# Norms of 512 tokens by per-token sums: root and reciprocal on 128x4, then spread over all rows by a matmul

## The reference, cut to what matters

```python
def _rmsnorm(x, g):
    x32 = x.astype(jnp.float32)
    y = x32 * lax.rsqrt(jnp.mean(x32 * x32, axis=-1, keepdims=True) + RMS_EPS)
    return y.astype(x.dtype) * g
def _modnorm(x, g_pre, shift, scale):
    return _rmsnorm(x, g_pre) * (1 + scale) + shift
def _residual(x, y, g_post, gate, weight):
    return x + weight * gate * _rmsnorm(y, g_post)
```

## Time and profile before

| | us |
|---|---|
| median of 3 runs | 3153.08 |
| lowest and highest | 3149.70 and 3153.67 |
| the profiled execution | 3148.06 |
| its span, first to last instruction | 3146.4 |
| PE busy in it | 2970.6 (94%) |
| DVE busy | 1012.7 (32%) |
| ACT busy | 448.3 (14%) |
| POOL busy | 393.4 (13%) |
| mean granted clock of PE | 0.981 of full |

### The profile page before, as it was taken

How to read it: one execution, slowest core, us unless ns; L and a number is a source line. 1 busy time by engine, 2 the same in 40 slices (tenths; PEclk the granted TensorE clock), 3 DMA queues, 4 the chain that set the end, 5 groups by cost and what they waited for, 6 DMA issues and landing times.

```text
span 3146.4 us, 27449 instructions
## 1 busy us (share of the span) xinstructions
PE 2970.6 (94%) x10974; PEld 1869.7 (59%) x10974; DVE 1012.7 (32%) x1970; ACT 448.3 (14%) x966; POOL 393.4 (13%) x355
## 2 busy tenths in 40 slices
PE   3999999998899999998999998999889999999998
PEld 1555555554456557443688884656444444888863
DVE  6233324202204633011533235205541002544432
ACT  2000000001103335001210001004430000000011
POOL 0000000000001000001244430000000001444410
PEclk8999999999999999999999999999999999999999
DMA  6233223211110000221122221120002221222211
GB/s 258 81 107 107 94 102 109 101 55 40 54 53 16 22 31 1 70 87 67 67 83 91 84 77 67 67 69 28 28 27 87 71 76 67 81 94 81 94 49 59
DMA packets 42526, 228.17 MB, mean 73 GB/s; under 512 B 4144, under 2 KB 6448, under 8 KB 26928
## 3 DMA queue, kind: packets, MB, share of 16 engines
q1 hardware_dynamic: 32768, 181.17, 17.0%
q0 software_dynamic: 8928, 39.85, 3.5%
q10 hardware_dynamic: 720, 5.61, 0.4%
HBM read 224.51 MB, written 2.10 MB: 72 GB/s over the span
## 4 chain that ended last, share of the span: by engine, by line
PE 91%; DVE 5%; ACT 1%; DMA 1%; issue 1%; POOL 0%; ACTq 0%; DVEq 0%
PE banks L413 57%; PE banks L489 24%; PE banks L601 2%; PE banks L422 1%; DMA consts_sb<-consts 1%; PE banks L773 1%; PE banks L689 1%; PE banks L781 1%; PE banks L926 1%; DVE rstd L1371 1%; DVE p_embed L1421 1%; DVE scratch_b L1388 1%; PE banks L702 1%; PE banks L774 0%; DVE rstd L1381 0%
## 5 line engine op out<-in xcount | busy, mean ns | idle before, releaser
L413 PE MATMUL banks<-normed,weight_ring 128*128 128x512 f32 (+1 forms) x3056 | 1150.4, 537 | 53.4 <-ACT normed L1007 34.0
L413 PEld LDWEIGHTS banks<-normed,weight_ring 128*128 128x128 f32 (+1 forms) x3056 | 582.3, 191 | 610.2 <-issue 564.7
L413 PE MATMUL banks<-big,weight_ring 128*128 128x512 f32 (+2 forms) x1504 | 572.0, 538 | 8.5 <-DVE big L1619 5.6
L413 PEld LDWEIGHTS banks<-big,weight_ring 128*128 128x128 f32 (+2 forms) x1504 | 279.3, 186 | 294.3 <-issue 272.7
L489 PE MATMUL banks<-big 128*128 128x256 f32 x1440 | 331.7, 379 | 0.0
L489 PEld LDWEIGHTS banks<-big 128*128 128x128 f32 x1440 | 273.6, 190 | 37.2
L1984 POOL TENSOR_TENSOR big<-weight_ring 128x512 f32<-128x512 f32 (+1 forms) x64 | 80.0, 1250 | 1176.4 <-PE banks L489 478.3
L489 PE MATMUL banks<-big,weight_ring 128*128 128x256 f32 x840 | 196.3, 379 | 0.0
L489 PEld LDWEIGHTS banks<-big,weight_ring 128*128 128x128 f32 x840 | 159.6, 190 | 21.7
L1421 DVE CUSTOM_DVE_ANT_0 p_embed<-big,rpb_rows 128x1024 f32<-128x1024 f32 x116 | 141.9, 1223 | 22.8 <-DMA big<-w_ada 14.8
L489 PE MATMUL banks<-normed,weight_ring 128*128 128x256 f32 x576 | 136.1, 379 | 0.0
(11 more groups left out here) (286 smaller groups left out, 2407.2 us busy)
## 6 DMA issues: line engine op xcount, KB each, us to landing
weight_ring<-weights SPq DMA_DIRECT2D x136, 1024.0 KB, 4.9
big<-w_ada POOLq DMA_DIRECT2D x42, 512.0 KB, 4.1
weight_ring<-weights SPq DMA_DIRECT2D x20, 768.0 KB, 4.2
weight_ring<-weights SPq DMA_DIRECT2D x16, 704.0 KB, 4.0
big<-w_ada POOLq DMA_DIRECT2D x4, 2048.0 KB, 24.9
rpb_rows<-w_ada POOLq DMA_DIRECT2D x14, 512.0 KB, 4.7
weight_ring<-weights SPq DMA_DIRECT2D x8, 640.0 KB, 3.9
residual<-xT ACTq DMA_DIRECT2D x2, 1536.0 KB, 19.7
```

Of the source, the lines that this page charges most:

```text
L413: ins = nc.tensor.matmul(o, w, r, start=start, stop=stop)
```

## The change

For the seven norms of 512 tokens the sums are turned round: each 128x128 block of squares is the stationary operand and one column of ones the moving one, so that the sums of 128 tokens come out as one column, token on partition, and the four blocks fill four columns. Root and reciprocal then work on 128x4. To get 1/root back onto every row, DVE multiplies the identity by each of the four columns, which makes four diagonal matrices side by side in `DIAG`, and one matmul of ones by `DIAG` puts the value of token t in column t of every row of bank 7 (`spread`). The scaling reads bank 7 in place of `rs`. Norms that cover the context too (two parts) are left as they were.

```diff
+        diag_made, spread_done = sem("rstd_diagonals"), sem("rstd_spread")
+        SPREAD = ("nb_y", "nb_x", "nmix_y", "nmix_x", "nmlp_x", "nple_x", "nfin_x")
@@ PE: sum_squares
+                if len(parts) == 1:
+                    return token_sums(banks[0], SQ[:, k % 2, 0:S], k == 0, k == count - 1)
+            def token_sums(n, rows, start, stop):
+                for c in range(4):
+                    last = nc.tensor.matmul(bank[:, n, c:c + 1], rows[:, c * P:(c + 1) * P], ones[:, 0:1],
+                                            start=start and c == 0, stop=stop, skip_group_check=True)
+                return last
+            def spread(name):
+                pe.wait_ge(diag_made, SPREAD.index(name) + 1)
+                nc.tensor.matmul(bank[:, 7, :], ones, DIAG[:, :, :].rearrange("p c t -> p (c t)"), start=True,
+                                 stop=True).then_inc(spread_done, 1)
@@ PE: out_chunks (and in the same way in out_projection)
-                        for (a, b, _), q in zip(parts, banks):
-                            last = nc.tensor.matmul(bank[:, q, 0:b - a], ones, SQ[:, 1 - j, a:b],
-                                                    start=(peel and j == 1), stop=False)
-                        last.then_inc(sg["sq_used"], 1)
+                        token_sums(banks[0], SQ[:, 1 - j, 0:S], peel and j == 1, False).then_inc(sg["sq_used"], 1)
@@ PE: squares_total
-                nc.tensor.matmul(bank[:, 6, :], ones, SQA[:, 0:S], start=True, stop=False)
-                nc.tensor.matmul(bank[:, 6, :], ones, SQA[:, S:2 * S], start=False, stop=False)
+                token_sums(6, SQA[:, 0:S], True, False)
+                token_sums(6, SQA[:, S:2 * S], False, False)
...
@@ PE: a spread after the sums of each of the seven norms, as in
+            spread("nb_y")
             norm_sums(nb, LAT)
+            spread("nb_x")
@@ ACT: root
+                if len(parts) == 1:
+                    A(rs[:, 0:4], bank[:, banks[0], 0:4], ACT.Sqrt, bias=eps, scale=1.0 / features).then_inc(signal, 1)
+                    return
@@ DVE: norm and post_norm call this, and scale by r in place of rs
+            def inverse_root(parts, name):
+                if len(parts) == 2:
+                    link(V.reciprocal(rs[:, :], rs[:, :]))
+                    return rs
+                link(V.reciprocal(rs[:, 0:4], rs[:, 0:4]))
+                V.tensor_tensor(DIAG[:, :, :], ident.unsqueeze(1).to_broadcast([P, 4, P]),
+                                rs[:, 0:4].unsqueeze(2).to_broadcast([P, 4, P]), ALU.mult).then_inc(diag_made, 1)
+                dve.wait_ge(spread_done, SPREAD.index(name) + 1)
+                return bank[:, 7, :]
```

More of the change, by code:

```diff
@@ L537, in squares_total @@
                 pe.wait_ge(g["added"], 2 * g["turn"] + 2)
-                nc.tensor.matmul(bank[:, 6, :], ones, SQA[:, 0:S], start=True, stop=False)
-                nc.tensor.matmul(bank[:, 6, :], ones, SQA[:, S:2 * S], start=False, stop=False)
+                token_sums(6, SQA[:, 0:S], True, False)
+                token_sums(6, SQA[:, S:2 * S], False, False)
                 pe.wait_ge(g["done"], 4 * g["turn"] + 4)
-                nc.tensor.matmul(bank[:, 6, :], ones, SQB[:, 0:S], start=False, stop=False)
-                nc.tensor.matmul(bank[:, 6, :], ones, SQB[:, S:2 * S], start=False, stop=True).then_inc(g["used"], 1)
+                token_sums(6, SQB[:, 0:S], False, False)
+                token_sums(6, SQB[:, S:2 * S], False, True).then_inc(g["used"], 1)
             def out_projection(g, free, name, tiles, rhs, parts, per_unit, sums):
@@ L555, in out_projection @@
                     pe.wait_ge(sg["sq_used"], sg["base"] + KC - 1)
-                    for (a, b, _), q in zip(parts, banks):
-                        nc.tensor.matmul(bank[:, q, 0:b - a], ones, TMP[:, 0, a:b], start=True, stop=False)
-                    pe.wait_ge(sg["sq"], sg["base"] + KC)
-                    for (a, b, _), q in zip(parts, banks):
-                        last = nc.tensor.matmul(bank[:, q, 0:b - a], ones, SQ[:, 1, a:b], start=False, stop=True)
+                    if len(parts) == 1:
+                        token_sums(banks[0], TMP[:, 0, 0:S], True, False)
+                    else:
+                        for (a, b, _), q in zip(parts, banks):
+                            nc.tensor.matmul(bank[:, q, 0:b - a], ones, TMP[:, 0, a:b], start=True, stop=False)
+                    pe.wait_ge(sg["sq"], sg["base"] + KC)
+                    if len(parts) == 1:
+                        last = token_sums(banks[0], SQ[:, 1, 0:S], False, True)
+                    else:
+                        for (a, b, _), q in zip(parts, banks):
+                            last = nc.tensor.matmul(bank[:, q, 0:b - a], ones, SQ[:, 1, a:b], start=False, stop=True)
                     last.then_inc(sg["sq_used"], 1)
@@ L805, in _ @@
             squares_total(sq2)
+            spread("nmix_y")
             norm_sums(nmix, LAT)
+            spread("nmix_x")
             for b in range(8):
@@ L941, in _ @@
             out_projection(out2, nmlp["xnew"], "out2", KC, MR2, LAT, 16, (nmlp, (6,)))
+            spread("nmlp_x")
             first_up(UP3[0], (V_UP3[1] + 1) % 2, nmlp)
@@ L952, in _ @@
             squares_total(sq3)
+            spread("nple_x")
             pe.wait_ge(p_landed, 16)
@@ L972, in _ @@
                 sum_squares(nfin, o, LAT, (6,)).then_inc(nfin["sq_used"], 1)
+            spread("nfin_x")
         @block.scalar
@@ L1366, in mark, with norm, post_norm @@
                 return chain[0]
-            def norm(g, parts, scale, shifted):
+            def inverse_root(parts, name):
[7 more added lines that the diff above has]
+                return bank[:, 7, :]
+            def norm(g, parts, scale, shifted, name=None):
                 dve.wait_ge(g["root"], g["turn"] + len(parts))
-                width = parts[-1][1]
-                link(V.reciprocal(rs[:, 0:width], rs[:, 0:width]))
+                r = inverse_root(parts, name)
                 for k in range(KC):
                     for a, b, col in parts:
-                        V.scalar_tensor_tensor(H[:, k, a:b], X[:, k, a:b], scale(k, col), rs[:, a:b], ALU.mult,
+                        V.scalar_tensor_tensor(H[:, k, a:b], X[:, k, a:b], scale(k, col), r[:, a:b], ALU.mult,
                                                ALU.mult).then_inc(g["scaled"] if shifted else g["ready"], 1)
-            def post_norm(g, parts, gate_row):
+            def post_norm(g, parts, gate_row, name=None):
                 dve.wait_ge(g["y_root"], len(parts))
-                width = parts[-1][1]
-                link(V.reciprocal(rs[:, 0:width], rs[:, 0:width]))
+                r = inverse_root(parts, name)
                 marks = {}
@@ L1772, in _ @@
             dve.wait_ge(out1["free"], 2 * KC)
-            post_norm(nb, LAT, GATE2)
-            norm(nb, LAT, modulated(SCALE3), True)
+            post_norm(nb, LAT, GATE2, "nb_y")
+            norm(nb, LAT, modulated(SCALE3), True, "nb_x")
             dve.wait_ge(nb["ready"], KC)
@@ L1790, in _ @@
                     add_squares(sq2, m - 1)
-            post_norm(nmix, LAT, GATE3)
-            norm(nmix, LAT, plain("mix_g"), False)
+            post_norm(nmix, LAT, GATE3, "nmix_y")
+            norm(nmix, LAT, plain("mix_g"), False, "nmix_x")
             for b in range(8):
@@ L1917, in _ @@
             residual_adds(nmlp, out2["done"])
-            norm(nmlp, LAT, plain("mlp_g"), False)
+            norm(nmlp, LAT, plain("mlp_g"), False, "nmlp_x")
             XA, XB = X[:, :, 0:HALF], X[:, :, HALF:S]
@@ L1933, in _ @@
                     add_squares(sq3, m - 1)
-            norm(nple, LAT, plain("ple_g"), False)
+            norm(nple, LAT, plain("ple_g"), False, "nple_x")
             for o in range(KC):
@@ L1940, in _ @@
                 V.tensor_tensor(X[:, o, 0:S], X[:, o, 0:S], TMP5[:, s, :], ALU.add).then_inc(nfin["xnew"], 1)
-            norm(nfin, LAT, plain("final_g"), False)
+            norm(nfin, LAT, plain("final_g"), False, "nfin_x")
         @block.gpsimd
```

2 lines of the change are left out of this document (1 added, 1 removed).

## The result

The changed kernel took 3159.23 us (median of 20 executions, 3157.36 to 3163.27), the kernel before 3152.61 (20 executions). The ratio is 1.0023, with a 95% interval of 1.0016 to 1.0030: 6.6 us slower, where 12.0 us faster was forecast.

What follows compares the result with a forecast made beforehand. The prediction took the uncovered root, reciprocal and scaling at seven norms as the bound, with PE busy 94%. Gains of 6.8 + 2.4 + 1.0 + 1.8 = 12.0 us from the median 3153.1 gave 3141 us, range 3131 to 3148.

Steps and rivals of the forecast that it cites:

- What bounds the kernel: At the seven norms of 512 tokens, root, 3.35 us reciprocal and scaling run one by one, 4.11 us at nmlp_x, uncovered.
- The relay, new: Root to scaling at seven norms: 2.42 us at full clock, 3.43 at half, against 4.11; five spreads at half, gain 6.8 us.
- The sums: the price of a pair: On PE, a weight load plus one-column pass takes 0.08 us, so 0.64 us a sum, 0.22 less than a wide one.
- path term: Sums between matmuls of out2 and the last projection: 11 x 0.22, gain 2.4 us (ends 4.0 and -1.1).
- the sums fit under it: In nb_x and nmix_x, sums (0.64, or 0.96 at half clock) fit under DVE's 1.39 us a chunk; gain 1.0 us.
- nmix_y and nple_x: Two small sums follow ACT's square ahead of the root, which starts earlier; gain 0.9 us each, 1.8 us together.
- The stage behind the norm: First matmuls behind norms start earlier but no warmer: 0; ends 5.6 us gained if clock stays up, 2.8 lost.
- The gain is eaten by half speed: Rival: all spreads at half clock, dearer sums, 2.8 us lost behind norms; 1.5 us gain, 3151.6 us, chance 0.07.
- Slower: Rival: in small sums load and pass don't overlap, 0.19 us a pair at full clock, twice at half; 3180 us, chance 0.04.

Runs made afterwards that it cites:

- rsqrt: The kernel before, with root and reciprocal of the seven norms replaced by one ACT instruction for the reciprocal square root; 3118.89 us, ratio 0.9896.
- narrow_loops: The changed kernel with one-column sums only in the loops nb_x and nmix_x and wide sums everywhere else; 3143.99 us, ratio 0.9983 to the kernel before.
- relay_alone: The changed kernel with all sums kept wide, so only root and reciprocal on 128x4, diagonals and spread are new; 3134.74 us, ratio 0.9949 to the kernel before.
- narrow_and_wide: The changed kernel with one unread wide matmul added behind each narrow sum of nb_x and nmix_x; 3177.17 us, ratio 1.0082 to the kernel before.

## Why the prediction was wrong, step by step

The shifts between the two traces, sorted by the terms of the forecast (us, minus is faster):

| term | forecast | measured |
|---|---|---|
| seven relays, root to scaling | -6.8 | -6.2 |
| sums on PE's path | -2.4 | +0.4 |
| loops of nb_x and nmix_x, first sum to root | -1.0 | +6.9 |
| four sums of nmix_y and of nple_x, to the root | -1.8 | +3.0 |
| stages behind the norms | 0 | +3.4 |
| first two chunks of out2 | none | +3.0 |
| sum | -12.0 | +10.5 |

The last term is the scatter named above, and the one before it may hold some too; the medians differ by +6.6.

- *What bounds the kernel* was right: seven reciprocals of 3.35 us on the path, with PE waiting. rsqrt takes them off it and gives 33 us, with the clock behind them.
- *The relay, new.* Forecast 2.42 us at full clock and 3.43 at half; measured 2.49 (nb_y) and 3.36 (nb_x). The small root took 0.26 (0.25 forecast), the reciprocal 0.18 (0.18), the diagonals 0.69 (0.68), the spread with its hand-over 1.17 or 2.11. Right in every term. Six spreads, not five, ran at half clock.
- *The sums: the price of a pair.* I took 0.08 us by L899. L433's loads start 0.11 us apart at full clock (eight fill 0.97, the last of them 0.19 long) and 0.21 at half (25 fill 5.41), so a sum is 0.89 and 1.71, not 0.64 and 0.96. The path term became a loss of about 0.4 (11 x 0.04, by the steps of out2). The section "LDWEIGHTS (loading the stationary operand)" of the Trainium skill's page "TensorE: Matmul & The Clock Gate", which I had set against the trace, says that a load takes its columns divided by 1.2 in ns, an estimate of 107 ns for 128. At full clock L433's 112 ns lie near it; at half clock they are 213. L899's four-row loads, nearer by their moving columns, were the wrong neighbour, and why they follow each other at 0.06 no run shows. The full-sized loads of L689 were the right one at full clock: sixteen in 1.86 us, the last about 0.19 long, are 0.11 apart and not the 0.12 that I read.
- *nb_x and nmix_x: "the sums fit under it".* This is the step that failed. I priced the loop at half clock by a guess for the pair (0.96 a sum), and did not double the full-clock length, as the wide matmul does in my own rows (1.13 to 2.17). At 1.71 a sum PE paces the loop in place of DVE's 1.39. The worse part: before the change the loop, too, started at half clock, and its wide sums brought the clock up in its second half. I counted the narrow sums as light work when I chose the clock of the spread, but did not ask what the loop would lose if they are light there. In place of 1.0 us of gain the two loops lost 3.4 and 3.5: nb_x goes from 1.66 us ahead at its first sum to 1.72 behind at its root. This is the largest difference of the table.
- *nmix_y and nple_x.* Forecast 0.9 us of gain each. By the chain, the four sums took 4.02 and 6.39 us, with wide sums 3.71 and 3.72 (narrow_loops). A loss instead, and for the same reason: at nple_x nearly all of them ran at half clock.
- *The stage behind the norm.* I took 0 and said it would not be warmer. In the change it was at half clock for longer than before behind nb_x and nmix_x (by 1.2 us each); relay_alone shows that with wide sums it would have been at full there, 1.7 us less than before each. I had allowed for both as ends of the range, but tied neither to the sums.
- *The rivals.* "The gain is eaten by half speed" came nearest in mechanism, at 3151.6 and a chance of 0.07, but kept the loops paced by DVE. "Slower" named the right place and the right test ("it decides from about 0.15 us a pair, where the loops begin to bind"). It priced the pair by the full length of a load, 0.19, at full clock and put the loops at 2.7 us a chunk, which gave 3180. The pair is at 0.11 when the clock is full and over 0.15 only where the clock is at half. I gave it 0.04, since I looked for the excess in the overlap of load and pass and not in the clock.

## What to carry to other kernels

When small matmuls replace a wide one, ask which clock they will run at and which they will leave, and price them at both. Here a pass that moves one column took as long as one that moves 128 (0.11 and 0.21 us at the two levels), but the loop of the first stayed at half clock and that of the second came up. What PE does right ahead of a short relay on other engines decided the clock behind it as well: after wide sums all seven spreads were at full, after narrow ones one. And before a costly operation is made smaller by a change of layout, look whether another engine has it as part of an operation that stands beside it already (here 1/root for root, at the same 0.69 us).

## What the runs showed of the hardware that I had not expected

Pairs of a 128x128 weight load and a narrow pass, on 32-bit data, start 0.112 us apart at full clock and 0.213 at half, with 1, 64 or 128 moving columns; the 64 pairs of nb_x took 13.83 us with one column and 13.93 with 64, all at half. In narrow_and_wide PE was busy for 27.3 of 28 us, more than half of it in wide matmuls, and the granted clock stayed at 0.50 for all of it. In the kernel before, wide sums alone started at half at 1496.41, and the clock was 1.00 from 1503 on.
